# Where a norm's additions run: all on VectorE, none on GpSimd, and two weight splits placed ahead of the norm

## The reference

```python
def _rmsnorm(x, g):
    y = x * lax.rsqrt(jnp.mean(x * x, axis=-1, keepdims=True) + RMS_EPS)
    return y * g

def _swiglu(h, w_in, w_out):
    a = h @ w_in
    return (jax.nn.silu(a[..., :FFN_HIDDEN]) * a[..., FFN_HIDDEN:]) @ w_out

for i in range(DEPTH):            # DEPTH = 4
    m = mixer_i(_rmsnorm(x, norm_w[i, 0]))     # retention, convolution, attention, retention
    x = x + _rmsnorm(m, norm_w[i, 1])
    f = _swiglu(_rmsnorm(x, norm_w[i, 2]), ffn_w_in[i], ffn_w_out[i])
    x = x + _rmsnorm(f, norm_w[i, 3])
```

## Time and profile before

| | us |
|---|---|
| median of 3 runs | 2631.46 |
| lowest, highest | 2627.93, 2633.34 |
| the profiled execution | 2630.0 |
| its span | 2628.2 |
| PE busy in the span | 2473.3 (94%) |
| DVE busy | 1763.7 (67%) |
| ACT busy | 1338.8 (51%) |
| POOL busy | 62.1 (2%) |

### The profile page before, as it was taken

How to read it: one execution, slowest core, us unless ns; L and a number is a source line. 1 busy time by engine, 2 the same in 40 slices (tenths; PEclk the granted TensorE clock), 3 DMA queues, 4 the chain that set the end, 5 groups by cost and what they waited for, 6 DMA issues and landing times.

```text
span 2628.2 us, 54097 instructions
## 1 busy us (share of the span) xinstructions
PE 2473.3 (94%) x18779; PEld 2353.0 (90%) x18779; DVE 1763.7 (67%) x3431; ACT 1338.8 (51%) x2813; POOL 62.1 (2%) x73
## 2 busy tenths in 40 slices
PE   7999998989999999999999899998997999988998
PEld 7888998979998999889988899988886999877998
DVE  6556666977656776776575566655776775677764
ACT  4535555556554444465555355544664444454443
...
GB/s 204 183 89 152 190 197 121 100 80 161 199 169 113 122 125 122 105 166 192 200 144 185 88 158 186 196 156 122 136 120 81 168 176 174 123 93 92 175 176 128
DMA packets 103380, 385.39 MB, mean 147 GB/s; under 512 B 11344, under 2 KB 13392, under 8 KB 103024
## 3 DMA queue, kind: packets, MB, share of 16 engines
...
q0 software_dynamic: 496, 2.24, 0.2%
...
...
## 4 chain that ended last, share of the span: by engine, by line
PE 84%; DVE 10%; ACT 3%; issue 2%; DMA 0%; POOL 0%; DVEq 0%; ACTq 0%; SPq 0%; POOLq 0%
PE acc L494 24%; PE acc L496 23%; PE acc L495 23%; DVE weights_lo L1586 2%; PE acc L646 2%; PE acc L601 1%; PE acc L630 1%; PE acc L632 1%; PE acc L631 1%; PE acc L537 1%; PE acc L684 1%; PE acc L725 1%; PE acc L814 1%; PE acc L705 1%; DVE xn_parts L1690 1%
## 5 line engine op out<-in xcount | busy, mean ns | idle before, releaser
L1586 DVE TENSOR_TENSOR weights_lo<-weights,weights_hi 128x512 fp32r<-128x512 f32 (+1 forms) x1392 | 926.0, 698 | 448.0 <-ACT weights_hi L1039 442.2
L494 PE MATMUL acc<-xn_parts,weights_hi 128*128 128x256 f32 (+1 forms) x3456 | 997.8, 289 | 48.8 <-DVE xn_parts L1690 19.5
L495 PE MATMUL acc<-xn_parts,weights_hi 128*128 128x256 f32 (+1 forms) x3456 | 981.5, 284 | 0.0
L496 PE MATMUL acc<-xn_parts,weights_lo 128*128 128x256 f32 (+1 forms) x3456 | 981.3, 284 | 0.0
L1039 ACT ACTIVATE weights_hi<-weights 128x512 fp32r<-128x512 f32 (+1 forms) x1392 | 810.7, 620 | 259.5 <-PE acc L496 230.8
L494 PEld LDWEIGHTS acc<-xn_parts,weights_hi 128*128 128x128 f32 x3456 | 657.0, 190 | 67.9 <-issue 52.1
L495 PEld LDWEIGHTS acc<-xn_parts,weights_hi 128*128 128x128 f32 x3456 | 659.2, 191 | 1.2
L496 PEld LDWEIGHTS acc<-xn_parts,weights_lo 128*128 128x128 f32 x3456 | 657.1, 190 | 0.0
L494 PE MATMUL acc<-arena_r,weights_hi 128*128 128x256 f32 (+1 forms) x1792 | 514.5, 287 | 16.1 <-DVE weights_lo L1586 9.5
L495 PE MATMUL acc<-arena_r,weights_hi 128*128 128x256 f32 (+1 forms) x1792 | 510.4, 285 | 0.0
L496 PE MATMUL acc<-arena_r,weights_lo 128*128 128x256 f32 (+1 forms) x1792 | 510.4, 285 | 0.0
...
## 6 DMA issues: line engine op xcount, KB each, us to landing
...
```

Source lines behind the costliest of these rows:

```text
L494: nc.tensor.matmul(acc, hi, src_hi, start=first, stop=False)
L495: nc.tensor.matmul(acc, hi, src_lo, start=False, stop=False)
L496: return nc.tensor.matmul(acc, lo, src_hi, start=False, stop=last)
L1586: nc.vector.tensor_tensor(w_lo[sub % phase.subs][:, 0:n, :], raw[slot][:, j * SUB:j * SUB + n, :], w_hi[sub % phase.subs][:, 0:n, :].bitca ...
```

## The change

The 14 POOL additions of each norm are taken out. DVE now adds x[c] + y[c] for all eight chunks in `split_residual`, right behind each `scale`, and adds up the squares in `gated_pairs`, between its splits of unit 0 (subs 8, 9) and unit 1 (subs 10, 11) of the second turn. Sub 2 (unit 1, part 0) is now split at the end of the mixer's output phase, behind subs 0 and 1; sub 3 (unit 1, part 1) is split by ACT between its last read of the mixer's output and the making of rstd, and by DVE just ahead of its wait for rstd. The splits of subs 4 to 7 are placed anew. The lines of the two files differ by some tens: line 1586 of before is line 1569 of the changed kernel, 1686 is 1671, 1690 is 1675, 1697 is 1680, and on ACT 1039 is 1029, 1104 and 1105 are 1096 and 1097, 1152 and 1153 are 1144 and 1145, and 1184 and 1185 are 1176 and 1177.

```diff
--- before.py
+++ after.py
@@ -76,6 +76,7 @@
     loads, split = [0] * SLOTS, [0] * SLOTS
     for ph, after in zip(seq, seq[1:] + [None]):
         ph.out0, ph.pair0, ph.sub0, ph.after = out, pair, sub, after
+        ph.chunkwise = ph.name.startswith("ffn_in")
         if after:
             after.before = ph
         ph.loads0, ph.split0 = list(loads), list(split)
@@ -455,17 +456,6 @@
         def _(pool):
             pool.dma_start(h[:, :, 0:META], dram["meta"]).then_inc(meta_loaded, 16)
             pool.dma_start(w_gates[:, :, :], dram["ab_gates"]).then_inc(meta_loaded, 16)
-            for layer in range(DEPTH):
-                posts, first = DC * (2 * layer), DC * (2 * layer + 1)
-                for c in range(1, DC):
-                    pool.wait_ge(scaled, posts + c + 1)
-                    nc.gpsimd.tensor_tensor(x[:, c, :], x[:, c, :], y[:, c, 0:S1], ALU.add).then_inc(x_ready, 1)
-                for c in range(1, DC):
-                    pool.wait_ge(squares_ready, first + c + 1)
-                    if c > 1:
-                        pool.wait_ge(square_summed, FREE_SQUARES + first + c)
-                    nc.gpsimd.tensor_tensor(square_sum, squares[:, 0, :] if c == 1 else square_sum, squares[:, c, :], ALU.add)\
-                        .then_inc(square_summed, 2 if c == 1 else 1)
             pool.wait_ge(x_ready, 2 * DEPTH * DC)
             pool.dma_start(cb[:, 0:sum(n for _, n in at_c.values())], dram["const_c"]).then_inc(consts2_loaded, 16)
             pool.dma_start(w_r, dram["lru_w_r"]).then_inc(consts2_loaded, 16)
@@ -1055,6 +1045,8 @@
                         split(phase, turns - 1, u + 1)
                     elif phase.after:
                         split(phase.after, 0, 0)
+                        if phase.after.chunkwise:
+                            split_part(phase.after, 0, 1, 0)
                     unit(turns - 1, u)
 
             def wait_unit(phase, i, u):
@@ -1184,20 +1176,10 @@
                     nc.scalar.activation(xn_hi[S1][:, c, :], x[:, c, :], ACT.Copy, scale=param("norm_w", col + c)).then_inc(xh_ready, 1)
                     nc.scalar.activation(squares[:, c, :], x[:, c, :], ACT.Square).then_inc(squares_ready, 1)
 
-                split_part(phase, 0, 1, 0)
-                chunk(0)
-                split_part(phase, 0, 1, 1)
-                chunk(1)
-                chunk(2)
-                split_part(phase, 0, 2, 0)
-                chunk(3)
-                split_part(phase, 0, 2, 1)
-                chunk(4)
-                chunk(5)
-                split_part(phase, 0, 3, 0)
-                chunk(6)
-                split_part(phase, 0, 3, 1)
-                chunk(7)
+                for c in range(DC):
+                    chunk(c)
+                    if c in (2, 3, 5, 6):
+                        split_part(phase, 0, *{2: (2, 0), 3: (2, 1), 5: (3, 0), 6: (3, 1)}[c])
 
             def gated_pairs(phase, layer):
 
@@ -1534,6 +1516,7 @@
                     attention()
                     decay()
                     evacuate_y(4 * layer + 1, ph["att_out"])
+                split_part(ph[f"ffn_in{layer}"], 0, 1, 1)
                 post_norm(4 * layer + 1, S1)
                 split_residual(layer, ph[f"ffn_in{layer}"])
                 gated_pairs(ph[f"ffn_in{layer}"], layer)
@@ -1690,32 +1675,21 @@
                     stt(xn_lo[S1][:, c, :], x[:, c, :], param("norm_w", col + DC + c), xn_hi[S1][:, c, :].bitcast(F32),
                         ALU.mult, ALU.subtract).then_inc(x_split, 1)
 
+                def add(c):
+                    dve.wait_ge(scaled, posts + c + 1)
+                    nc.vector.tensor_tensor(x[:, c, :], x[:, c, :], y[:, c, 0:S1], ALU.add).then_inc(x_ready, 1)
+
+                split_part(phase, 0, 1, 1)
                 dve.wait_ge(rstd_ready, k + 1)
                 dve.sem_inc(y_added, 1)
-                scale(0)
-                dve.wait_ge(scaled, posts + 1)
-                nc.vector.tensor_tensor(x[:, 0, :], x[:, 0, :], y[:, 0, 0:S1], ALU.add).then_inc(x_ready, 1)
-                scale(1)
-                scale(2)
-                rest(0)
-                split_part(phase, 0, 1, 0)
-                scale(3)
-                rest(1)
-                split_part(phase, 0, 1, 1)
-                scale(4)
-                rest(2)
-                scale(5)
-                rest(3)
-                split_part(phase, 0, 2, 0)
-                scale(6)
-                rest(4)
-                split_part(phase, 0, 2, 1)
-                scale(7)
-                rest(5)
-                split_part(phase, 0, 3, 0)
-                rest(6)
-                split_part(phase, 0, 3, 1)
-                rest(7)
+                for c in range(DC):
+                    scale(c)
+                    add(c)
+                    if c:
+                        rest(c - 1)
+                    if c in (3, 4, 6, 7):
+                        split_part(phase, 0, *{3: (2, 0), 4: (2, 1), 6: (3, 0), 7: (3, 1)}[c])
+                rest(DC - 1)
 
             def post_norm(k, col):
 
@@ -1802,6 +1776,13 @@
 
                 turns = phase.units // phase.body
                 split(phase, 1, 0)
+                first = DC * (2 * layer + 1)
+                for c in range(1, DC):
+                    dve.wait_ge(squares_ready, first + c + 1)
+                    if c > 1:
+                        dve.wait_ge(square_summed, FREE_SQUARES + first + c)
+                    nc.vector.tensor_tensor(square_sum, squares[:, 0, :] if c == 1 else square_sum, squares[:, c, :], ALU.add)\
+                        .then_inc(square_summed, 2 if c == 1 else 1)
                 split(phase, 1, 1)
                 split(phase, 1, 2)
                 dve.wait_ge(rstd_ready, 4 * layer + 3)
```

## The result

| | before | changed |
|---|---|---|
| median of 7 runs, us | 2631.71 | 2612.51 |
| lowest, highest | 2627.93, 2634.79 | 2600.96, 2619.39 |
| ratio, with its 95% interval | | 0.9923 [0.9902, 0.9944] |
| the profiled execution | 2630.0 | 2600.96 |
| its span | 2628.2 | 2599.2 |

The change gains 19 us where 7.5 were forecast. The profiled execution of the changed kernel is the fastest of its seven.

The account below looks back on a forecast made before the run. DVE, slowed by POOL, was taken to pace the four norms, with PE late next. Gains of 2.0 + 3 x 1.5 = 6.5 us gave 2623.5 from the profiled execution, 2625 from the median; 2624 was taken, range 2618 to 2630.

Parts of the forecast that it names:

- The remainders and `rest`: DVE in the norms, sign of being right: weight remainders of 0.69 us and `rest` of 0.47 throughout.
- The pitches 0.52, 0.34 and 0.39: DVE, start to start in us: `scale` to the addition needing it, addition to the next instruction, and `rest`.
- Chunk 0: PE's start on chunk 0 in norm 1: 246.25 instead of 246.66, a gain of 0.4 us.
- the moved splits: Splits of subs 2 and 3 moved forward: free on DVE while it waits for rstd, no cost on ACT.
- slower: Rival, 2637 us: long DVE remainders come from something that stays, such as ACT's or PE's reads; chance 0.07.
- given back: Rival, 2627 us: ACT's waits for PE and DVE's longer list leave 1 to 3 us in all; chance 0.24.
- the norms, 4.6 us for 6.5: Gain over the four norms: 2.0 us in norm 1 and 1.5 in each of three others, 6.5 in all.
- not late: Sum of squares on DVE: seven additions at 0.46 us, ready at 261.4, PE ending unit 0 at 261.6.
- a sign of being wrong: PE waiting for the sum of squares, listed among what would show the prediction wrong.
- the 0.27 of the forecast: Unit 1 waits for DVE's split of sub 10, starting some 0.27 us after PE could.
- 12.65 and three times 13.35: Chunk 0 to unit 0, us: norm 1, then norms with half clock on chunk 0; granted clock 0.88 assumed.
- what lies behind unit 1: New norm's rstd and gates come 0.3 us later against unit 1, first needed by unit 3: cost nothing.

Follow-up runs that it names:

- the second trace: The kernel before, unaltered, run once more for a second trace: 2633.15 us, ratio 1.0006.
- the extra matmul: Changed kernel plus 16 unread f32 matmuls like the squares' one in the ffn_out phases, PE waiting for each: 2628.04 us, ratio 0.9984.

## Why the prediction was wrong

**Right: DVE and POOL.** The remainders and `rest` fell to 0.69 and 0.48 throughout the norm. The pitches 0.52, 0.34 and 0.39 stand in the rows above to 0.01. Chunk 0 came 0.41 us earlier against the first `scale`, as worked out, and the way from the mixer's last product to that `scale` was the same to 0.01 us in norm 1: the moved splits cost nothing there. The rival "slower", by which the long remainders had another cause, falls. So does "given back", which left 1 to 3 us: ACT waits for PE 4.1 us in norm 1, in six pieces, not 5.7.

**Off in size: the norms, 4.6 us for 6.5.** The same gain was 3.6, 5.0 and 4.3 in the three other traces of the changed kernel, against 91.9. Three terms of the first trace:

- An addition of squares has a pitch of 0.50, not 0.46: seven took 258.38 - 254.86 = 3.52 us for 3.2. So the sum was late after all, where the prediction had "not late" and named such a wait as a sign of being wrong: in norms 1 to 3 PE waited 0.2 us ahead of the squares' matmul.
- Unit 1 then started 0.60 us behind that matmul, not 0.51: 0.36 later than an unbroken stream, for the 0.27 of the forecast.
- From chunk 0 to unit 0 it took 13.14, 14.03, 13.11 and 13.39, for 12.65 and three times 13.35. Norm 2 has a granted clock of 0.82 over the stretch, where the forecast took 0.88.

**The step that failed: what lies behind unit 1 was put at "nothing".** In the prediction's words the new norm's rstd and its gates "are first needed by unit 3, two units of 2.7 us on: nothing." The prediction followed what the stop for sub 10 delays, found nobody waiting, and closed the account at unit 1. It took for granted that PE behind unit 1 runs as before. In fact 1464 products stand behind it in each layer, and the pitch of the 936 in `ffn_in` is settled at this very place. The 0.27 us that the sum booked as a cost are what took the squares' matmul out of an unbroken stream, and so brought 4.2 us per layer in `ffn_in`: three of four phases were long before (all four in the second trace), and 3, 4 and 3 of four were short in the other traces of the changed kernel, 4 in the first. So two to four phases fewer ran long, which is 8 to 17 us. The medians missed 11.7 us (19.2 for 7.5), and 13.6 with the 1.9 by which the norms fell short: the same size.

The figure was to be had. The prediction used 24 matmuls in 2.73 us, 114 ns each, from a stretch at the short pitch, ahead of the squares' matmul; 766 matmuls in 90 us behind it are 117.5. Nobody who compares the two can hold that PE at a clock of 1.00 has one speed. The range was built from bounds on the norms' own terms, and no rival had a mechanism outside them.

**What stays open.** What in PE makes the two pitches isn't known; the runs show only when they come, and the pairs of f32 matmuls in layer 2's attention, with the short pitch behind them 34 times out of 34, show that U isn't the whole of it. U fits all 32 cases at 0.24, of which 10 could tell, but explains neither why two of 28 were long at 0.60, nor why all 16 were long at 0.93: those lie in `ffn_out`, where the products around the extra matmul read other tiles and come out of a loop's turn, and that was not taken apart. Whether the distance counts or the stop itself isn't separated either. The pitch of `ffn_out` is settled anew 33 products in, where PE stops for 0.2 us behind a long `ffn_in` and for 0.45 behind a short one. Behind a long `ffn_in` it was long 13 times and short 14, behind a short one 9 and 24, over 15 traces. What decides there was not tried. The changed kernel's medians, 2612.5, 2622.0, 2609.7 and 2611.9 on four chips, differ by more than its norms do (under 1.5 us); the traces put it on the pitch in places such as these and on the granted clock in the stretch ahead of norm 3, but whether the chip has a part in it is open. The first trace of the changed kernel, with all eight pitches short and that stretch at 1.00, is the fastest of its seven runs and no typical one.
